# Second layer's modulation as row dot products on VectorE inside the first MLP; pooling windows moved into the input projection; three output-weight blocks split one phase earlier

## What is computed

```python
mod = silu(c) @ ada_w[layer] + ada_b[layer]      # 6 * 1024 numbers; the same for c_ctx
u = rmsnorm(h, norm1) * (1 + sc1) + sh1
z = u @ w_in                                     # layer 0: 768 pooling columns za, 256 Fourier columns zb
pooled = mean_over_window(za) - za               # windows 2, 4, 8, 16, by group of 192 channels
y = concat(pooled @ pool_w * pool_scale, real(fft2(zb)) @ fourier_w) @ w_out
h = h + gt1 * y
h = h + gt2 * mlp(rmsnorm(h, norm2) * (1 + sc2) + sh2)
```

## Time and profile before

| | us |
|---|---|
| median of 3 runs | 3353.41 (3348.68 to 3943.93) |
| the profiled execution | 3356.53 |
| its span | 3354.7 |
| TensorE busy in the span | 3150.1 (94%) |
| start_phase | 0 to 206.1 |
| pool_fourier_phase | 207.0 to 322.6 |
| output projection and first MLP | 323.4 to 1366 |

### The profile page before, as it was taken

How to read it: one execution, slowest core, us unless ns; L and a number is a source line. 1 busy time by engine, 2 the same in 40 slices (tenths; PEclk the granted TensorE clock), 3 DMA queues, 4 the chain that set the end, 5 groups by cost and what they waited for, 6 DMA issues and landing times. The chain is left out here.

```text
span 3354.7 us, 64953 instructions
## 1 busy us (share of the span) xinstructions
PE 3150.1 (94%) x28106; PEld 2555.2 (76%) x28106; DVE 1531.8 (46%) x2364; ACT 814.7 (24%) x1585; POOL 878.5 (26%) x495
## 2 busy tenths in 40 slices
PE   5897999999999999999969799999969999999999
PEld 4653887888888888788857577777758788888887
DVE  4053344443444444712256566767745444434434
ACT  4011121000000000310145566666622211011000
POOL 3200323333333333243211100000014533343342
PEclk8998999999999999999989899999979999999999
DMA  5455101111111011022120101111021111111111
GB/s 229 151 190 220 44 26 44 38 38 39 38 39 38 33 38 38 26 99 85 60 75 11 50 27 34 31 29 32 15 74 51 47 48 51 38 56 50 44 50 69
DMA packets 70870, 200.67 MB, mean 60 GB/s; under 512 B 8145, under 2 KB 26833, under 8 KB 70482
## 3 DMA queue, kind: packets, MB, share of 16 engines
q1 hardware_dynamic: 67154, 182.22, 16.1%
q10 hardware_dynamic: 3456, 14.55, 1.1%
HBM read 175.90 MB, written 20.84 MB: 59 GB/s over the span
## 5 line engine op out<-in xcount | busy, mean ns | idle before, releaser
L155 POOL TENSOR_TENSOR w_hi<-w_raw,zero 128x1024 fp32r<-128x1024 f32 x158 | 304.0, 1924 | 1263.0 <-PE ps L167 804.5
L167 PE MATMUL ps<-u_hi,w_hi 128*128 128x512 f32 (+1 forms) x2232 | 602.2, 369 | 13.4 <-POOL w_lo L158 9.1
L167 PE MATMUL ps<-u_lo,w_hi 128*128 128x512 f32 (+1 forms) x2232 | 600.3, 369 | 0.0
L167 PE MATMUL ps<-u_hi,w_lo 128*128 128x512 f32 (+1 forms) x2232 | 599.9, 368 | 0.0
L787 DVE SCALAR_TENSOR_TENSOR ffn_cv<-ps,small,ffn_cv 128x1023 f32<-128x1023 f32 (+1 forms) x132 | 134.1, 1016 | 770.4 <-ACT ffn_cv L1138 768.8
L167 PEld LDWEIGHTS ps<-u_hi,w_hi 128*128 128x128 f32 x2232 | 387.1, 188 | 94.8 <-issue 15.2
L167 PEld LDWEIGHTS ps<-u_hi,w_lo 128*128 128x128 f32 x2232 | 387.4, 188 | 73.1
L167 PEld LDWEIGHTS ps<-u_lo,w_hi 128*128 128x128 f32 x2232 | 387.3, 188 | 73.2
L1138 ACT ACTIVATE ffn_cv<-ps,small 128x1280 f32<-128x1280 f32 (+1 forms) x88 | 107.8, 1225 | 1238.9 <-PE ps L167 1227.4
L158 POOL TENSOR_TENSOR w_lo<-w_raw,w_hi 128x1024 fp32r<-128x1024 f32 x158 | 383.2, 2425 | 12.4
L631 DVE SCALAR_TENSOR_TENSOR h<-ps,mod,h 128x1024 f32<-128x1024 f32 x210 | 206.6, 1013 | 140.6 <-PE ps L1087 140.1
(11 more groups left out here) (364 smaller groups left out, 4866.4 us busy)
## 6 DMA issues: line engine op xcount, KB each, us to landing
w_raw<-in_ffn SPq DMA_DIRECT2D x132, 512.0 KB, 3.3
ada_ring_t<-in_ada SPq DMA_DIRECT2D x20, 512.0 KB, 6.0
w_raw<-in_cd_in SPq DMA_DIRECT2D x20, 512.0 KB, 4.1
z_scratch<-cd_stage ACTq DMA_DIRECT2D x15, 640.0 KB, 5.3
ada_ring<-in_ada SPq DMA_DIRECT2D x18, 512.0 KB, 6.1
ada_first<-in_ada SPq DMA_DIRECT2D x16, 512.0 KB, 15.6
ada_ring_s<-in_ada SPq DMA_DIRECT2D x14, 512.0 KB, 5.5
ada_ring_w<-in_ada SPq DMA_DIRECT2D x14, 512.0 KB, 6.5
```

Of the source, the lines that this page charges most:

```text
L155: pool.tensor_tensor(hi, K.raw[:, raw, :], K.zero[:, 0:1].to_broadcast([P, KT * P]), ALU.add).then_inc(self.hi_done, 1)
L167: mm = pe.matmul(K.ps[:, slot, c, 0:width], wt[:, s, w], x[:, k, at:at + width], start=start and n == 0, stop=stop and n == 2)
```

## The change

1. start_phase: the ring of modulation pieces has 3 buffers; pieces are spread singly over the k of tiles 2, 3, 5 and 6 (29 bursts of one, after a first burst of three). SP issues pieces 0 to 2, blocks 2 to 6, pieces 3 to 11, block 7, the rest. POOL splits block 2 after the first chunk's remainders. G is made within tile 2 in two halves. VectorE makes the pooling windows of tile t once it is evicted, latent and context tokens apart.
2. pool_fourier_phase: no G, no windows, none of the 48 pieces, no transposes. SP loads and POOL splits output blocks 0 to 2 there, and the output projection starts with them.
3. First MLP, in the loop: ScalarE's queue loads 64 tiles of 128x1024 (one tile is 128 output features with 1024 weights each) into two buffers; VectorE makes 64 dot products along the rows (`dve_dot`), r = 0 to 3 after the four up tiles of a group, r = 4 to 7 after down tiles 2, 3, 5 and 7. Ahead of the last down VectorE adds the bias and forms the gains (`dve_finish`).

```diff
+ABOUT_FIRST = 3
...
-    RING = 5
+    RING = 3
     spare = K.place("ada_ring_s", [P, 2, 1024], F32, at=K.s_at + 41728)
-    ring = K.place("ada_ring", [P, 3, 1024], F32, at=K.ring_at)
-    row2 = K.place("ada_row", [P, 512], F32, at=K.ring_at + 12288)
+    ring = K.place("ada_ring", [P, 1, 1024], F32, at=K.ring_at + 12416)
+    row2 = K.place("ada_row", [P, 512], F32, at=K.s_at + 24 * PW + 4 * NT)
...
-    bursts = {(1, 7): 5, (2, 7): 5, (3, 3): 3, (3, 7): 3, (4, 7): 5, (5, 7): 5, (6, 3): 3, (6, 7): 3}
+    mats_in, g_done, g_out, win_own = [K.sem(x) for x in ("dft_mats_in", "dft_g_done", "dft_g_out", "pool_win_own")]
+    windows = {0: [(0, 128, 2)], 1: [(0, 64, 2), (64, 128, 4)], 2: [(0, 128, 4)],
+               3: [(0, 128, 8)], 4: [(0, 64, 8), (64, 128, 16)], 5: [(0, 128, 16)]}
+    bursts = {(1, 7): 3}
+    for m, ks in ((2, range(1, 8)), (3, (1, 2, 3, 5, 6, 7)), (4, (7,)), (5, range(1, 8)), (6, range(8))):
+        for k in ks:
+            bursts[m, k] = 1
...
-            for n in range(RING):
+            sp.dma_start(mats[:, :, :, :], a["dft_ch"]).then_inc(mats_in, 16)
+            def piece(n):
+                if n >= RING:
+                    sp.wait_ge(piece_used, n - RING + 1)
                 sp.dma_start(piece_of(n), a["ada"][1 + n // 16, n % 16]).then_inc(piece_in[n % RING], 16)
-            for b in range(2, KT):
+            def weights(b):
                 sp.wait_ge(W.split, b - 1)
                 sp.dma_start(K.raw[:, b % 2, :], a["ab_in"][b]).then_inc(W.loaded[b % 2], 16)
-            for n in range(RING, 32):
-                sp.wait_ge(piece_used, n - RING + 1)
-                sp.dma_start(piece_of(n), a["ada"][1 + n // 16, n % 16]).then_inc(piece_in[n % RING], 16)
+            for n in range(RING):
+                piece(n)
+            for b in range(2, 7):
+                weights(b)
+            for n in range(RING, 12):
+                piece(n)
+            weights(7)
+            for n in range(12, 32):
+                piece(n)
...
-            for n in range(3):
+            for n in range(2):
                 W.divide_one(pool, n % 2, n % 3, n, n // 2)
             for c in range(3):
                 for k in norm.POOL_KS:
                     norm.pool_lo(pool, c, k)
+                if c == 0:
+                    W.divide_one(pool, 0, 2, 2, 1)
...
+                if m == 2:
+                    for half in range(2):
+                        act.wait_ge(g_done, half + 1)
+                        act.copy(K.dft_g[:, half, :], K.ps[:, 1, 3, :]).then_inc(g_out, 1)
...
+                    if (m, k) == (2, 0):
+                        channels(0)
+                    if (m, k) == (2, 4):
+                        pe.wait_ge(g_out, 1)
+                        channels(1)
                     if m in (4, 7) and k == 5:
                         pe.wait_ge(row_out, 2 if m == 4 else 3)
+                        if m == 4:
+                            pe.wait_ge(g_out, 2)
...
-            for quad in (1, 2):
+            own = Chain(dve, win_own)
+            edge = K.S("edge").rearrange("p (w s e) -> p w s e", w=4, s=2)
+            dve.wait_ge(zeroed, 3)
+            def pool_windows(t, p0, p1, w):
+                wi = w.bit_length() - 2
+                for at, size in zip(ZA_AT, (SEQ, CTX)):
+                    cur, n, s, b = za[p0:p1, t, at - 8:at + size + 8], size + 16, 1, 0
+                    while s < w:
+                        n -= s
+                        nxt = win[p0:p1, b, :]
+                        own.link(dve.tensor_tensor(nxt[:, 0:n], cur[:, 0:n], cur[:, s:s + n], ALU.add))
+                        cur, s, b = nxt, 2 * s, 1 - b
+                    first = 8 - w // 2
+                    ends = cur[:, first:first + size].rearrange("p (s e) -> p s e", e=8)[:, ::size // 8 - 1, :]
+                    own.link(dve.tensor_tensor(ends, ends, edge[p0:p1, wi, :, :], ALU.mult))
+                    own.link(dve.scalar_tensor_tensor(za[p0:p1, t, at:at + size], cur[:, first:first + size], 1.0 / w,
+                                                      za[p0:p1, t, at:at + size], ALU.mult, ALU.subtract))
+            def quad_mods(quad):
                 dve.wait_ge(turned, quad + 1)
                 ada_mods(dve, K, K.ps[:, 1, 3, :], quad).then_inc(mod_done, 1)
+            for t in range(6):
+                if t == 4:
+                    quad_mods(1)
+                dve.wait_ge(stored, t + 1)
+                for piece in windows[t]:
+                    pool_windows(t, *piece)
+            quad_mods(2)
...
+        self.ready = ABOUT_FIRST if y_dram is None else 0
...
-        if c == 0:
-            pe.wait_ge(self.split, m + 1)
+        if c == 0 and m >= self.ready:
+            pe.wait_ge(self.split, m - self.ready + 1)
...
+class ModRows:
+    DOTS = 64
+    DOWN_AT = {2: 4, 3: 5, 5: 6, 7: 7}
+    def __init__(self, K):
+        self.K = K
+        self.cond = K.place("ada_cond_rows", [P, 2, D], F32, at=K.ring_at)
+        self.tile = K.place("ada_tile", [P, 2, D], F32, at=K.ring_at + 8192)
+        self.cond_in, self.tile_in = K.sem("ada_cond_in"), [K.sem(f"ada_tile_in{s}") for s in range(2)]
+        self.dots, self.biased, self.gains = K.sem("ada_dots"), K.sem("ada_biased"), K.sem("ada_gains2")
+    def act_load_cond(self, act):
+        act.dma_start(self.cond[:, :, :], self.K.a["cond_rows"]).then_inc(self.cond_in, 16)
+    def act_silu(self, act):
+        act.wait_ge(self.cond_in, 16)
+        act.activation(self.cond[:, :, :], self.cond[:, :, :], ACT.Silu).then_inc(self.dots, 1)
+    def act_load(self, act, e, r):
+        act.wait_ge(self.dots, 8 * e + max(r, 1))
+        act.dma_start(self.tile[:, r % 2, :], self.K.a["ada_rows"][8 * e + r]).then_inc(self.tile_in[r % 2], 16)
+    def dve_dot(self, dve, e, r):
+        at = 96 + (4 * e + r if r < 4 else 32 + 8 * e + 2 * (r - 4))
+        col = self.K.mod.rearrange("p l t c -> p (l t c)")[:, bass.ds(at, 1)]
+        dve.wait_ge(self.tile_in[r % 2], 64 * e + 16 * (r // 2 + 1))
+        if r == 0:
+            dve.wait_ge(self.dots, 1)
+        t = self.tile[:, r % 2, :]
+        dve.scalar_tensor_tensor(t, t, 1.0, self.cond[:, r % 2 if r < 4 else 0, :], ALU.mult, ALU.mult,
+                                 accum_out=col).then_inc(self.dots, 1)
+    def over(self, eng):
+        eng.wait_ge(self.dots, 1 + self.DOTS)
+    def dve_finish(self, dve):
+        K = self.K
+        bias = K.S("ada_b")[:, 48:96]
+        self.over(dve)
+        dve.tensor_tensor(K.mod[:, 1, :, 0], K.mod[:, 1, :, 0], bias, ALU.add).then_inc(self.biased, 1)
+        dve.tensor_tensor(K.mod[:, 1, 0:16, 1], K.mod[:, 1, 0:16, 1], bias[:, 0:16], ALU.add).then_inc(self.biased, 1)
+        dve.wait_ge(self.biased, 2)
+        gains_of(dve, K, 2)
+        gains_of(dve, K, 3, (0,)).then_inc(self.gains, 1)
+        dve.wait_ge(self.gains, 1)
...
+                if mods is not None:
+                    mods.over(pool)
...
+            def looped(g):
+                return mods is not None and not isinstance(g, int)
             def up(g, par):
+                if looped(g):
+                    mods.act_load(act, g - 2, 0)
+                    mods.act_load(act, g - 2, 1)
...
+                    if looped(g):
+                        mods.act_load(act, g - 2, q + 2)
+                if mods is not None and isinstance(g, int):
+                    if g == 0:
+                        mods.act_load_cond(act)
+                    if g == 1:
+                        mods.act_silu(act)
+            def down(g, par):
+                if looped(g):
+                    mods.act_load(act, g - 1, 6)
+                    mods.act_load(act, g - 1, 7)
...
-            schedule(up, lambda g, par: None, act)
+            schedule(up, down, act)
             if nxt is not None:
+                mods.over(act)
...
+                    if mods is not None and not isinstance(g, int):
+                        mods.dve_dot(dve, g - 2, q)
...
+                    if mods is not None and not isinstance(g, int) and m in mods.DOWN_AT:
+                        mods.dve_dot(dve, g - 1, mods.DOWN_AT[m])
             def down_end():
+                if mods is not None:
+                    mods.dve_finish(dve)
...
-            sp.dma_start(mats[:, :, :, :], a["dft_ch"]).then_inc(mats_in, 16)
-            def piece(n):
-                if n >= RING:
-                    sp.wait_ge(piece_used, n - RING + 1)
-                sp.dma_start(piece_of(n), a["ada"][3 + n // 16, n % 16]).then_inc(piece_in[n % RING], 16)
             for t in range(FT4):
                 sp.dma_start(tab[:, t, :, :], a["dft_tok"][t]).then_inc(tab_in[t], 16)
-                piece(t)
...
+            for m in range(ABOUT_FIRST):
+                if m >= 2:
+                    sp.wait_ge(next_lo, m - 1)
+                sp.dma_start(K.raw[:, m % 2, :], a["ab_out"][m]).then_inc(next_in[m % 2], 16)
+        @block.gpsimd
+        def _(pool):
+            for m in range(ABOUT_FIRST):
```

(30 more changed lines are left out.)

127 lines of the change are left out of this document (36 added, 91 removed).

## The result

The changed kernel takes 3341.2 us (median of 14 runs, 3330.7 to 3350.2) against 3353.4 for the kernel before in the same sessions: ratio 0.9967, interval [0.9958, 0.9976]. That is 12.2 us less, where 28.9 were forecast. It is inside the forecast range, at its slow end. The profiled execution took 3341.46 us with a span of 3339.7 us, 15.0 less than the kernel before's 3354.7.

The account below looks back on a forecast made before the run. TensorE, busy 94% of the span, was taken as the bound. Terms -31.2 (Fourier phase), -8.5 (projection), +0.5 (start_phase), +10 (first MLP) and +0.3 (dve_finish) summed to -28.9, forecasting 3325 us, range 3309 to 3342.

Parts of the forecast that it names:

- half-rate dot: Rival, first MLP: VectorE's dot needs two passes over its fp32 operands, 8 to 16 us more; chance 0.15.
- the bound of the ya tiles: pool_fourier_phase: TensorE stays the bound at 4.5 us for its shortest tile, ScalarE and VectorE following in under 4.5.
- I take +2.0: pool_fourier_phase: TensorE's first products run at a low clock after some 5 us of idleness, costing +2.0 us.
- 29 x 0.95 = +27.6: start_phase: 29 modulation pieces issued singly cost TensorE 0.95 us each, as long as pairs, +27.6 us in all.
- singles are cheap: Rival, start_phase: TensorE overlaps a single piece with products around it, 0.5 us each, total 3312 us; chance 0.10.
- wait for piece 3: start_phase, tile 2: piece 3, issued behind weight block 6, lands late and TensorE waits, +4.0 us (0 to 6).
- wait for POOL's remainder: start_phase: TensorE's wait while POOL splits block 2 goes, since that split moves behind the first chunk's remainders, -5.1 us.
- Neither bound: First MLP, dot r = 3 in 8 groups: 9 us from below, 18 from above with a second pass, at most 26.
- There nothing can be won, but much can be lost: First MLP, 428 to 1366 us: TensorE is already busy 929.1 of 938 us at the full granted clock.
- Five small instructions of 0.12 each: dve_finish, before the last down's first add: five short VectorE instructions and two waits, +0.3 us (0 to 1).
- pieces are late at every k: Rival, start_phase: three buffers hold only three k steps, chaining TensorE to the DMA, 8 us more, 3333; chance 0.05.
- the one that VectorE waits for tiles: Rival, first MLP: late layer 1 weight tiles stall VectorE before an add, making the kernel slower than before; chance 0.04.

Follow-up runs that it names:

- second execution: The changed kernel run and profiled once more with no edit: 3341.6 us, ratio 0.9955 to the kernel before.

## Why the prediction was wrong

28.9 us were forecast and 12.2 came. Three terms of the sum failed: the price of a single piece with the clock behind its wait (6.2 us in start_phase), the jumps back of the loop, which had no term at all (8.5), and dve_finish (3.5). That 3341 still lies in the stated range is luck: its slow end was made for a half-rate dot, and there is none.

- **pool_fourier_phase and the projection: right.** -31.2 and -8.5 were forecast, -30.4 and -8.3 measured. ScalarE's first eviction of yb, the bound of the ya tiles and the start 1 us behind the phase all came as worked out. The step "I take +2.0" for a low clock had about the right size: the 32 matmuls for which 7.17 was read took 8.81.
- **start_phase: the step "29 x 0.95 = +27.6" failed in its price.** Its mechanism was right: a single leaves as much time on the clock as a pair does. But a single costs 1.14, 5.5 us more over 29. The 0.95 was the third piece of a burst, 127.56 to 128.51, and a step inside a burst holds nothing of going in and out. A single's own step is 0.98, and another 0.16 falls on the product behind it. The rival "singles are cheap" was wrong in the other direction.
- The rest of start_phase: G cost 1.53 and 1.82 by its steps, not 2.0 each. The wait for piece 3 was 5.29 where 4.0 was forecast, and the sum had no term for the clock behind it, 2.2 us, though it had one in the Fourier phase. The wait for POOL's remainder went as said, and gave more than the 5.1: tile 1 came 6.9 us earlier. From 54.70 to 58.70 the granted clock was 0.50 behind that wait in the kernel before and is 1.00 now. Together 5.5 - 0.6 + 1.3 + 2.2 - 1.8 = 6.6, and 6.2 was measured.
- **The dots: right in mechanism and place.** One a group is paid in full: 1.04 and not 1.25, 8.4 and not 10. Neither bound held anything: no second pass over the operands. The dot's mean is 1.24 us, as the nearest relative's 1226 ns said, with 0.08 for its read of the accumulator behind it. The half rate that the Trainium skill's page named in the prediction gives for this kind isn't there in 64 dots.
- **The jumps back: a term that the sum hadn't got, +8.5.** "There nothing can be won, but much can be lost" was true, but I looked only for losses by the edits in the loop. This one comes from code that was taken out ahead of the loop. Nothing in the rows of before points to it but the 0.65 us with no releaser at one jump.
- **dve_finish: +0.3 became +3.8 (2.2 in the second execution).** "Five small instructions of 0.12 each" counted the instructions but not who runs beside them: one gain stood 2.29 us behind POOL, TensorE's wait of 2.0 us followed, and in the first execution the low clock behind that.
- The sum: -28.9 + 6.2 (start_phase) + 8.5 (jumps) + 3.5 (dve_finish) - 1.6 (dots) + 1.0 (the Fourier phase and the projection) = -11.3, and -12.2 was measured.
- The rival "pieces are late at every k" and the one that VectorE waits for tiles are not seen: one wait on a piece, none on a tile. The landing of ada_tile is 3.7 us in the median, under the 6.1 that I had taken.

## What to carry to other kernels

- A piece that fills half of the array costs as much as two side by side, so don't spread such pieces singly: 1.28 to 1.38 us for a pair against 1.14 for one. And take the price of a short operation between products from how far it moves the products on both sides apart, not from its own step: 0.16 of the 1.14 is not in that.
- When an edit changes how many instructions an engine has ahead of a loop, look at the first instructions behind each jump back for idle time without a releaser, and count the instruction packets there. Thirty-two instructions of padding gave some 10 us back.
- Tiny VectorE operations on a path want a place where POOL is idle. And a dot that stands ahead of an addition on which TensorE waits goes behind it.

## What the runs showed of the hardware that I had not expected

- A loop of TensorE, 171.7 us a round, either runs from what the engine holds (4 packets of 16 KB in 630 us) or is fetched anew each round (31), by where it starts. Fetched anew, a jump costs 0.3 to 0.9 us in the kernel before and, at the starts at which TensorE stands again three or six matmuls into the round, 2.1 to 5.9. That these starts lie just ahead of a block's end is what theory A says; no trace shows the blocks' ends.
- The gap behind a jump can take the clock down. It was 0.59 for 4 us behind the first gap of 2.22 us and 1.00 behind the second and third (1.83, 1.93) in one execution. With the pieces in pairs it was 0.50 behind gaps of 2.20 and 2.09 us. The groups then took 91.7 and 91.4 instead of 88.3 and 88.6. The same wait of 2.01 us at the MLP's end was followed by 0.58 in one execution of the changed kernel and by 1.00 in another. What decides it stays open.
- VectorE and POOL held each other up over SBUF: 2.29 us for an operation of 8 elements.
